# The value products of an attention loop: one key/value head at a time, 256 columns wide, in place of two heads by turns, 128 wide

## The reference, cut to what matters

```python
def latent_attention(qx, kx, vx, kc, vc):
    keys = jnp.concatenate([kc, kx], axis=1)      # 768 keys, 2 heads, 64 wide
    vals = jnp.concatenate([vc, vx], axis=1)
    qb = ...                                      # 4 blocks of 128 queries, 2 groups of 4 heads
    def block(q):
        s = jnp.einsum('bqkgd,bnkd->bkgqn', q, keys).astype(jnp.float32) * scale
        p = jax.nn.softmax(s, axis=-1)
        return jnp.einsum('bkgqn,bnkd->bqkgd', p.astype(vals.dtype), vals)
    return lax.map(block, qb)
```

## Time and profile before

| what | value |
|---|---|
| median of 3 runs | 2186.44 us |
| the profiled execution: time, span | 2186.44 us, 2184.8 us |
| TensorE busy in the span | 2043.5 us (94%) |
| VectorE, ScalarE busy | 1238.2 us (57%), 908.8 us (42%) |
| mean granted TensorE clock | 0.977 of full speed |
| V0 starts, last V starts | 1675.5 us, 1751.4 us |
| line 196 starts again (next layer) | 1754.8 us |

### The profile page before, as it was taken

How to read it: one execution, slowest core, us unless ns; L and a number is a source line. 1 busy time by engine, 2 the same in 40 slices (tenths; PEclk the granted TensorE clock), 3 DMA queues, 4 the chain that set the end, 5 groups by cost and what they waited for, 6 DMA issues and landing times. The chain is left out here.

```text
span 2184.8 us, 27379 instructions
## 1 busy us (share of the span) xinstructions
PE 2043.5 (94%) x9738; PEld 1629.6 (75%) x9738; DVE 1238.2 (57%) x1910; ACT 908.8 (42%) x1403; POOL 288.2 (13%) x380
## 2 busy tenths in 40 slices
PE   8999889999999999999999999789887898999997
PEld 6666556888888677688888867778765677888886
DVE  3666437788777646766664444676646644333333
ACT  4333535444422434444443245566437734222222
POOL 0032411000000111000000002666420001000000
PEclk9999999999999999999999999999998999999999
DMA  5511013566454322223333211110110022333321
GB/s 171 148 47 39 1 39 106 172 191 194 146 163 154 106 86 87 77 79 97 96 99 113 95 56 58 39 39 30 58 46 3 1 87 77 96 96 96 116 94 51
DMA packets 52782, 193.97 MB, mean 89 GB/s; under 512 B 5809, under 2 KB 8529, under 8 KB 52313
## 3 DMA queue, kind: packets, MB, share of 16 engines
q1 hardware_dynamic: 44824, 165.18, 23.8%
q0 software_dynamic: 7344, 27.27, 4.0%
q10 hardware_dynamic: 528, 0.40, 0.1%
HBM read 189.15 MB, written 3.68 MB: 88 GB/s over the span
## 5 line engine op out<-in xcount | busy, mean ns | idle before, releaser
L196 PE MATMUL psum<-xH,w_hi 128*128 128x512 f32 x1800 | 728.2, 405 | 42.1 <-DVE xL L1372 21.3
L196 PE MATMUL psum<-xL,w_hi 128*128 128x512 f32 x1800 | 711.1, 395 | 0.0
L196 PE MATMUL psum<-xH,w_lo 128*128 128x512 f32 x1800 | 710.8, 395 | 0.0
L166 DVE TENSOR_TENSOR w_lo<-w_raw,w_hi 128x1024 fp32r<-128x1024 f32 (+1 forms) x273 | 356.9, 1307 | 363.1 <-ACT w_hi L160 362.8
L160 ACT ACTIVATE w_hi<-w_raw 128x1024 fp32r<-128x1024 f32 (+1 forms) x273 | 303.4, 1111 | 416.7 <-PE psum L196 407.4
L196 PEld LDWEIGHTS psum<-xH,w_hi 128*128 128x128 f32 x1800 | 344.1, 191 | 140.1 <-DVE xL L1372 36.3
L196 PEld LDWEIGHTS psum<-xH,w_lo 128*128 128x128 f32 x1800 | 343.8, 191 | 73.7
L196 PEld LDWEIGHTS psum<-xL,w_hi 128*128 128x128 f32 x1800 | 344.6, 191 | 71.0 <-issue 3.1
L196 PE MATMUL psum<-hidH,w_hi 128*128 128x512 f32 x528 | 206.2, 391 | 0.0
L196 PE MATMUL psum<-hidH,w_lo 128*128 128x512 f32 x528 | 205.4, 389 | 0.0
L196 PE MATMUL psum<-hidL,w_hi 128*128 128x512 f32 x528 | 205.4, 389 | 0.0
(11 more groups left out here) (321 smaller groups left out, 2476.0 us busy)
## 6 DMA issues: line engine op xcount, KB each, us to landing
w_raw<-in_up SPq DMA_DIRECT2D x132, 512.0 KB, 3.5
w_raw<-in_down SPq DMA_DIRECT2D x48, 704.0 KB, 4.0
mod_raw<-in_mod POOLq DMA_DIRECT2D x48, 512.0 KB, 3.9
w_raw<-in_sb_in SPq DMA_DIRECT2D x26, 512.0 KB, 3.5
w_raw<-in_ev_in SPq DMA_DIRECT2D x23, 512.0 KB, 3.8
w_raw<-in_od_in SPq DMA_DIRECT2D x20, 512.0 KB, 3.5
w_raw<-in_ev_out SPq DMA_DIRECT2D x8, 512.0 KB, 3.6
w_raw<-in_od_out SPq DMA_DIRECT2D x8, 512.0 KB, 3.5
```

The lines of the kernel that those rows point to most:

```text
L166: nc.vector.tensor_tensor(w_lo[:, s % SPLIT, 0:w.cols], raw[:, s, 0:w.cols], w_hi[:, s % SPLIT, 0:w.cols].bitcast(F32), ALU.subtract).then ...
L196: mm = nc.tensor.matmul(acc, a[:, slot % SPLIT, cut], b[:, k0 + k, :], start=start and n == 0, stop=stop and n == 2)
```

## The change

In `logits` the unit number is read in another order. Before, `kv` alternates from unit to unit; now the four heads `r` of `kv` 0 come first and then those of `kv` 1. A pair `2n`, `2n + 1` therefore belongs to one key/value head. In `values` one matmul of 256 columns (two heads side by side in bank 7, both on the 64 partitions of their `kv`) stands where two of 128 columns stood, one on each half of the partitions. The layout of bank 7 at the end of a block is the same, and so is everything on VectorE and ScalarE.

```diff
                 def logits(u):
-                    i, r, kv = u // 8, (u // 2) % 4, u % 2
+                    i, kv, r = u // 8, (u // 4) % 2, u % 4
...
                 def values(n):
 
-                    r = n % 4
+                    kv, half = (n // 2) % 2, n % 2
...
                     for j in range(KT):
-                        for kv in range(2):
-                            mm = nc.tensor.matmul(bank[7][rows(kv), blk(r)], vall[:, j, kv * HD:(kv + 1) * HD],
-                                                  pT2[:, j, 2 * (n % 2) + kv, :], start=j == 0, stop=j == KT - 1)
+                        mm = nc.tensor.matmul(bank[7][rows(kv), half * 2 * P:(half + 1) * 2 * P], vall[:, j, kv * HD:(kv + 1) * HD],
+                                              pT2[:, j, 2 * half:2 * half + 2, :], start=j == 0, stop=j == KT - 1)
                     mm.then_inc(b["pv"], 1)
```

## The result

| | before | changed |
|---|---|---|
| median, us | 2186.88 (4 runs) | 2199.07 (4 runs) |
| range, us | 2186.41 to 2191.81 | 2198.18 to 2199.62 |
| span of the profiled execution | 2184.8 | 2196.9 |
| first logits row to the next layer's first row (L196) | 103.88 | 116.43 |

The changed kernel is slower: ratio 1.0052, 95% interval 1.0037 to 1.0066, which is 8 to 14 us; the medians lie 12.2 apart. The forecast was 2200.4, the range 2197.5 to 2205.

What follows compares the result with a forecast made beforehand. TensorE's own work and a chain of logits, reduce, exp and copies were taken to end rounds by turns. Longer value products +20.5, less 6.45 given back, made +14.0 on 2186.44: 2200.4 us, range 2197.5 to 2205.

Steps and rivals of the forecast that it cites:

- Two records to opposite halves run in the time of one: Value products on TensorE: the change leaves records without a partner, +1.28 us each, +20.5 for 16.
- V: One value product on TensorE in the attention loop, numbered V0 to V15; its slot was to grow from 1.46 to 2.74 us.
- The waits give back 6.45: TensorE's waits in the attention loop were to absorb 6.45 us of the +20.5, leaving +14.0.
- the first: Wait of the transposes at 1683.62, 1.49 us by start times: 1.27 given back.
- second: Wait of the transposes at 1688.82, 0.81 us: chain late by only 1.28, all 0.81 given back.
- third: Wait of the transposes at 1696.05, 2.84 us, its chain long by four extra VectorE operations: 0.47 given back.
- the four short ones: Four transposes with short waits, such as 1713.43: 0.28, 0.40, 0.30 and 0.30 us, all given back.
- the 1.2 GHz stretch before V4: Low clock between 1692.4 and 1701.1, around idle TensorE: price kept; without it -1.25 us.
- The order of the logits: Logits in the attention loop: only unit 1 changes, nothing taken; up to -1.6 us if its cover failed.
- Nothing given back: Rival: waits move with the value products, chain and products on one path; +20.5, 2206.9 us; 8%.
- Clock lower: Rival: half the array idle in value products, TensorE oftener at 1.2 GHz; about 2206.5 us; 6%.
- Not slower through overlap of any two records: Rival: records in value products overlap whatever their halves; slot 1.44 us, time 2186.1 us; 4%.

Runs made afterwards that it cites:

- wide products on two halves: Changed kernel with its 256-column products by turns on the two output halves, each holding part of the sum: 2186.04 us, ratio 0.9992 to before.
- narrow ones on one half: Changed kernel with each 256-column product split into two of 128 on the same half: 2199.45 us, ratio 1.0062 to before.
- heads in turn: Kernel before with the two value-product loops swapped, so six products for head 0, then six for head 1: 2197.65 us, ratio 1.0052.
- product twice: Kernel before with every value product computed twice, halves still by turns: 2198.79 us, ratio 1.0056.

## Why the prediction was right, point by point

- **Two records to opposite halves run in the time of one, and the change gives this up.** Right, and shown: wide products on two halves return to 1.45 us, narrow ones on one half stay at 2.76. The price from three other lines of the trace was 2.74 for V; measured 2.73. 16 x 1.27 = 20.4 against 20.5.
- **The waits give back 6.45.** The stage says 20.4 - 12.55 = 7.8, of which 1.25 is the clock (below): 6.6 by waits. Wait by wait, in start times, what remained: at the first 0.23 (predicted 0.22), second 0.57 (0), third 1.78 (2.37), at 1708.74 none (0), at 1719.47 0.67 (0.64), the four short ones none, V15 none. The waits of TensorE on ScalarE's copies and VectorE's scaling are 3.0 + 1.6 = 4.6 us, forecast about 5.
- **The second and third of these are the step that was off.** The transposes at 1688.82 were to wait no more, "chain late by only 1.28". But a chain also starts at V1's end, and this was 2.55 late: L, a reduce, VectorE's scaling and two gating operations, the next reduce, exp and the copies behind it take 7.3 us to 1690.78 in the changed kernel (from 1683.49), 7.5 before. The rows of the reduce in question are below. Before, it started at 1685.20, when VectorE (1685.09) and the L behind the late transposes (1685.16) had ended nearly together. After, it started behind VectorE's own work at 1687.18, 1.1 us after that L's end (1686.08). So of two chains that had tied, the one that I had left out became the last to end. That the sum was right in spite of it is luck: the next wait took the error back (0.57 more, 0.59 less).

```profile
1684.93 0.16 DVE L2466 RECIPROCAL stat<-stat 128x1 f32<-128x1 f32 x1
1685.20 0.96 DVE L2469 TENSOR_REDUCE stat<-psum 128x1 f32<-128x768 f32 x1
```

```profile
1684.50 0.96 DVE L2469 TENSOR_REDUCE stat<-psum 128x1 f32<-128x768 f32 x1 [2.04 <-PE psum L2652]
...
1687.18 0.94 DVE L2469 TENSOR_REDUCE stat<-psum 128x1 f32<-128x768 f32 x1
1688.15 0.90 ACT L2320 ACTIVATE probs<-psum,stat 128x768 f32<-128x768 f32 x1 [1.18 <-DVE stat L2469]
```

- **The clock.** I kept the price of the 1.2 GHz stretch before V4, and it was not paid: the clock from V3's end to V4 is 1.00. V4 lies 3.82 behind its transposes (1698.24 to 1702.06) and not 5.07: the 1.25 that I named as the low side. Forecast +14.0 less 1.25 gives 12.8, measured 12.55. Why it wasn't paid stays open. From V2's end to the transposes behind V3 TensorE was busy 5.5 of 8.8 us before (the row below) and 6.8 after, which speaks for a fuller TensorE. But in heads in turn it was busy 6.5 of 8.9 us, and the clock fell all the same, for longer. No run tests it alone, and the forecast named the gain only as its low side: that it came was luck, not foresight.

```profile
1687.21:1696.05 8.84, 5.53 (x50) 4.25 (x49) 7.74 (x14) 6.57 (x13) 0.00 (x0) 1.00 0.00 0
```

- **The order of the logits** cost and gained nothing: 103.81 against 103.88, wide on two halves against before. The wait of unit 1's logits went and the next one, for the exponential, grew.
- **The rivals.** Nothing given back (+20.5) is refuted by the stage's 12.55, and by 13.1 of 21.0 in product twice. Clock lower: the loop's mean went from 0.98 up to 1.00; the cost of 2.1 us in heads in turn shows that the price was real, though it fell on another kernel. Not slower through overlap of any two records: refuted by V's 2.73.

## What to carry to other kernels

When an output fills only half of the partitions, put its matmuls by turns on the two halves. In this kernel (fp32, 64 weight columns, 128 or 256 moving ones) TensorE then does two in the time of one, and a wider matmul on one half, with half as many instructions, throws that away for 5 ns each. Price such an edit by its slot in the trace, then walk the waits one by one from every earlier point that can feed them: a longer step cost more of its length than a shorter one gave back (62% and 37% here, the clock's part included). And a wait removed in a ring of engines is paid out in part by the next one: of 5.0 us, 3.1 arrived, and only with the neighbouring waits trimmed too did 6.5.

## What the runs showed of the hardware that I had not expected

- The overlap of opposite halves reaches past the neighbouring instruction: with twelve records on one half and then twelve on the other, about 3.5 of 24 slots of 0.109 us were saved around the change (V 2.38 us and not 2.77).
- A value matmul in fp32 shows as two records, 0.109 us each for 128 columns and 0.216 for 256 ((2.73 - 0.14)/12), so that in this stream an instruction costs almost nothing beyond its columns.
- What a stretch at 1.2 GHz costs depends on what lies in it. One of 3.4 us cost 1.25 before V4 in the kernel before, where V4's wait for its bank took a part back, and 1.3 when it met a value product (2.83 against 1.53 shown). One of 6.8 us cost 2.1 in heads in turn.
